# Forty tokens an expert instead of 48, and the second pair's weights fetched during attention

## The chip, the core and the metric

The kernel runs on one core of a Trainium2 chip. The metric is the device time of one execution in microseconds (us). Names of engines: PE is TensorE (its matmuls; PEld its weight loads), DVE is VectorE, ACT is ScalarE, POOL is GpSimd, SP is SyncE, which here only issues DMAs.

## The reference

Two blocks follow each other on 256 tokens of width 1024, all in float32. The first has two layers of retention and stick-breaking attention with a dense SwiGLU; the change does not touch it. The second has two layers of mixed attention followed by a mixture of 32 experts (4 groups of 8). Each token chooses the best group and in it the two best experts:

```python
lg = einsum('td,dg->tg', t, rg_w) + rg_b
g_star = argmax(lg, -1)
le = (einsum('td,gde->tge', t, re_w) + re_b) of the chosen group
top_v, top_i = lax.top_k(le, 2)
gate = p_top * softmax(top_v) at top_i
for g in range(4):
    h = silu(einsum('td,edf->tef', t, w_gate[g])) * einsum('td,edf->tef', t, w_up[g])
    y = y + einsum('tef,efd->td', h * gate[:, g, :, None], w_down[g])
```

Every expert has 1024 x 256 gate, 1024 x 256 up and 256 x 1024 down weights, 1 MB (1.049 million bytes) each. Worked out from the reference's own inputs, the fullest expert gets 30 tokens in the first of these two layers and 33 in the second.

## The kernel before

The experts are worked off in 16 pairs ("duos", `d` from 0 to 15), two experts at a time, side by side on the two halves of TensorE's columns. A pass serves at most `TAKEN_SLOTS` tokens of each expert; `npass` says at run time how many passes the fullest expert needs, and the kernel is built for up to `PASSES` of them, in nested branches. With at most 48 tokens each, one pass is enough.

In a pass PE does this for each pair (`moe_pass`, line 1720):

- `gather` (L1734): multiplies the tokens (in a high and a low part) with 0/1 columns of `pick`, `TAKEN_SLOTS` columns an expert, for a later group of pairs. The 16 pairs form five groups (`GROUP_DUOS`), of 2, 4, 4, 4 and 2 pairs; the columns of a whole group go through one matmul. A group of four pairs takes 32 matmuls of 8 x 48 = 384 columns, a group of two 32 matmuls of 4 x 48 = 192 columns. Group 0 is gathered before pair 0; group 1 during pairs 0 (24 matmuls) and 1 (8); group 2 during pairs 2 to 5, group 3 during 6 to 9 (8 matmuls in each pair), group 4 during 10 to 13 (8 in each, 192 columns). ACT (L2197) and DVE (L2915) copy the results to `XG`.
- `gate_up2` (L1775): the gate and up products of the pair, 16 matmul calls, which the profile counts as 32.
- `turn_hidden` (L1788) turns the hidden rows, ACT copies them (L2224); `turn_picks` (L1747, L1749) turns the picks for the scatter; `down2` (L1801) is the down product; `scatter` (L1815) adds the pair before to the tokens' sums in PSUM.

The gate and up matmuls always read 64 columns an expert (`SLOTS`), of which the last ones belong to the next expert and meet zero picks later.

**Weights.** A pair needs six units of 1 MB. There are 12 slots for them, six for even pairs (`ring`, slots 0 to 5) and six for odd ones: slots 6, 7 and 10 in `high`, slots 8, 9 and 11 in `more_slots`, a piece of the `arena`. For pairs 0 to 3 the gate and up weights come in halves of 0.5 MB (rows 0 to 3 and 4 to 7 of the eight), for the rest whole. SP issues every load of a weight, in order, on one queue. `expert_loads` (L1092) waits before each unit until PE has read what the slot held: for `d >= 2` the unit of pair `d - 2`; for pair 0, in the ring, the unit of `v1` or `w_o_2` of the attention; and before the first load of pair 1 there is one wait, on `z_dve` (L1105), DVE's signal that the second half of `Z`, the attention's normed output, is written. All ten loads of pair 1 (8 halves and 2 down units) stand behind it. `high` holds the high parts of the attention's weights until then (`high_part2`), and the arena holds the attention's tensors (`mqT`, `mkT`, `dqT`, `dkT` and others) in the places in which the expert stage keeps its own.

Of the kernel before, what the change touches and what calls it, by code (L numbers as in the profile page):

```python
# [32 lines left out]
P = 128  # L33
# [3 lines left out]
D = 1024  # L37
# [60 lines left out]
TAKEN_SLOTS = 48  # L98
# [238 lines left out]
def build(nc, src, out, debug=None):  # L337
# [7 lines left out]
    with ctx:  # L345
# [188 lines left out]

        arena_at[0] = moe_at
# [30 lines left out]
        pickT = carve(2, SEQ)  # L566
        Y = T8.rearrange("p k n -> p (k n)").rearrange("p (a n) -> p a n", a=2)
        H_high = carve(TT, D)
# [4 lines left out]
        more_slots = carve(EXPERT_SLOTS - RING - HIGH, UNIT)  # L573
        earlier_twins = len(twins)
        twin_of(gate_parts_flat, ident_moves, pick_flat, pickT, H_high)
# [5 lines left out]
        sg = carve(2, EH)  # L581
        hh = carve(2, EH)
        hT = carve(2, 2 * P)
# [340 lines left out]
        def expert_slot(name, d, i, h=0):  # L924

            if name == "down":
                return ring[:, 4 + i, :] if d % 2 == 0 else high[:, 2, :] if i == 0 else more_slots[:, 2, :]
            if d < HALVED:
                slot = ring[:, 2 * h + i, :] if d % 2 == 0 else high[:, i, :] if h == 0 else more_slots[:, i, :]
                return slot.rearrange("p (s k n) -> p s k n", s=2, k=KT // 2)  # L930
            slots = ring[:, 2 * i:2 * i + 2, :] if d % 2 == 0 else high[:, 0:2, :] if i == 0 else more_slots[:, 0:2, :]
            return slots.rearrange("p s (k n) -> p s k n", k=KT)

# [9 lines left out]
        def _(sp_):  # L943
# [116 lines left out]
            def wait_released2(key, l):  # L1060
                sp_.wait_ge(*released2(key, l))
# [3 lines left out]
            for l in range(LAYERS):  # L1065
# [25 lines left out]

                def expert_loads(pass_):  # L1092
                    passes = None
                    for d in range(DUOS):
                        if d == DUOS // 2 and pass_ == 0:
                            passes = passes_known()
                        for n, key in enumerate(duo_units(0, d)):
                            if d >= 2:
                                wait_released2(held_by(pass_, d - 2, units2[key]), l)
                            elif pass_ > 0:  # L1100
# [795 lines left out]
        def _(act):  # L1896
# [179 lines left out]
            for l in range(LAYERS):  # L2076
# [173 lines left out]
                def squares_of_rows():  # L2250

                    for t in range(TT):
                        act.wait_ge(mean_in.sem, mean_in.at(l, t + 1))
                        nc.scalar.activation(more_slots[:, 0, t * D:(t + 1) * D], H[:, t, :], ACT.Square,
                                             bias=less_mean[:, t:t + 1],
                                             accum_out=square_sum[:, t:t + 1]).then_inc(squares_in.sem, 1)
                    if l < LAYERS - 1:
                        high_parts2(0, 2, l + 1)
# [927 lines left out]
```

## Time and profile before

| | |
|---|---|
| median of 3 runs | 1687.33 us (1685.79 to 1688.91) |
| span of the profiled execution | 1686.1 us |
| what lies around the span | 1.2 us, taken as the median less the span; the profiled execution has no other time |
| PE busy | 1656.0 us, 98% of the span |
| DVE, ACT, POOL busy | 858.9, 652.7, 171.1 us |
| moved by DMA | 396.64 MB, 235 GB/s on average |
| expert stages | from about 1028 to 1262 us and from about 1438 to 1673 us |

The busy share of an engine over the whole span says little here, as the stages have different limits. A busy PE only says that matmuls were in flight. The views that bear on the change are the ones with times: the chain of waits, the stretches with the share of the DMA engines, SP's issues, and the time from a load's issue to its landing.

### The profile page before, as it was taken

How to read it: one execution, taken by the hardware profiler on the slowest of the kernel's cores; microseconds unless marked ns; L12 is line 12 of the kernel's file. 1: busy time of each engine (PE TensorE's matmuls, PEld its weight loads, DVE VectorE, ACT ScalarE, POOL GpSimd, SP SyncE). 2: the span in 40 equal slices, each digit the busy share in tenths (PEclk: the TensorE clock that was granted, in tenths of full speed). 3: DMA queues.
4: the chain of work that ended last, by engine and by line, in shares of the span. 5: the costliest groups of instructions: out<-in, count | busy, mean ns of one | idle time of the engine just before them, and what ended most of it. 6: DMA issues, size and time to landing. Idle time of an engine off the chain costs nothing. (4 is left out here: it accounts for less than half of the span.)

```text
span 1686.1 us, 23648 instructions
## 1 busy us (share of the span) xinstructions
PE 1656.0 (98%) x9477; PEld 1260.6 (75%) x9477; DVE 858.9 (51%) x1418; ACT 652.7 (39%) x920; POOL 171.1 (10%) x242
## 2 busy tenths in 40 slices
PE   9999999999999999999999999999999999999996
PEld 6888879999798887999988975444548887544453
DVE  6466564444646556544457856322127785532223
ACT  4465444343446554433344553111115554211111
POOL 2020001111102000111111040000002122000000
PEclk9999999999999999999999999999999999999998
DMA  8544545553754454555366528999995624999995
GB/s 316 176 149 144 181 150 185 190 185 114 242 183 132 143 181 169 175 188 186 124 203 192 170 76 312 409 423 423 423 394 180 194 101 136 355 425 423 423 423 211
DMA packets 156285, 396.64 MB, mean 235 GB/s; under 512 B 20496, under 2 KB 85008, under 8 KB 135696
## 3 DMA queue, kind: packets, MB, share of 16 engines
q1 hardware_dynamic: 156176, 395.18, 64.4%
q8 instruction: 69, 1.13, 0.3%
q14 instruction: 40, 0.33, 0.1%
HBM read 394.10 MB, written 1.05 MB: 234 GB/s over the span
## 5 line engine op out<-in xcount | busy, mean ns | idle before, releaser
L918 PE MATMUL ps<-split,split 128*128 128x256 f32 (+3 forms) x1872 | 631.2, 337 | 2.1 <-ACT split L1920 1.0
L922 PE MATMUL ps<-split,split 128*128 128x256 f32 (+3 forms) x1872 | 627.7, 335 | 0.2
L919 PE MATMUL ps<-split,split 128*128 128x256 f32 (+3 forms) x1872 | 623.7, 333 | 0.0
L896 DVE TENSOR_TENSOR split<-ring,split 128x2048 fp32r<-128x2048 f32 x136 | 313.6, 2313 | 253.0 <-ACT split L889 252.8
L918 PEld LDWEIGHTS ps<-split,split 128*128 128x128 f32 x1872 | 351.5, 188 | 37.4 <-DVE split L876 2.1
L922 PEld LDWEIGHTS ps<-split,split 128*128 128x128 f32 x1872 | 351.7, 188 | 35.8 <-DVE split L2302 1.3
L919 PEld LDWEIGHTS ps<-split,split 128*128 128x128 f32 x1872 | 352.9, 189 | 33.0 <-issue 0.5
L889 ACT ACTIVATE split<-ring 128x2048 fp32r<-128x2048 f32 x136 | 260.2, 1915 | 278.1 <-PE ps L922 269.4
L1775 PE MATMUL ps<-ring,arena 128*64 128x512 f32 x512 | 112.8, 592 | 0.0
L2952 DVE SCALAR_TENSOR_TENSOR arena<-arena,ps 128x256 f32<-128x256 f32 x32 | 15.4, 481 | 167.4 <-ACT arena L2219 131.9
L1775 PE MATMUL ps<-high,arena 128*64 128x512 f32 x256 | 98.8, 592 | 0.0
L1775 PE MATMUL ps<-arena 128*64 128x512 f32 x256 | 98.8, 592 | 0.0
L911 DVE TENSOR_TENSOR split<-ring,split 128x1536 fp32r<-128x1536 f32 (+3 forms) x44 | 80.7, 1852 | 25.7 <-ACT split L905 25.5
L2964 DVE TENSOR_TENSOR split<-ps,split 128x512 fp32r<-128x512 f32 x64 | 44.3, 692 | 95.8 <-ACT split L2226 95.8
L1775 PEld LDWEIGHTS ps<-ring,arena 128*64 128x64 f32 x512 | 38.5, 137 | 70.1 <-issue 70.1
L2219 ACT ACTIVATE arena<-ps 128x256 f32<-128x256 f32 x32 | 12.3, 384 | 200.5 <-PE ps L1775 200.5
L905 ACT ACTIVATE split<-ring 128x1536 fp32r<-128x1536 f32 (+3 forms) x44 | 67.7, 1546 | 49.1 <-PE ps L922 46.0
L2226 ACT ACTIVATE split<-ps 128x512 fp32r<-128x512 f32 x64 | 38.2, 597 | 111.7 <-PE ps L1801 111.7
L1775 PEld LDWEIGHTS ps<-high,arena 128*64 128x64 f32 x256 | 30.8, 137 | 62.0 <-issue 62.0
L1815 PE MATMUL ps<-split,split 128*128 128x512 f32 x240 | 62.5, 399 | 0.0
L1801 PE MATMUL ps<-ring,arena 128*64 128x512 f32 x256 | 58.5, 598 | 0.9 <-ACT arena L2224 0.9
L1801 PE MATMUL ps<-high,arena 128*64 128x512 f32 x128 | 58.2, 597 | 1.1 <-ACT arena L2224 0.9
(262 smaller groups left out, 1771.1 us busy)
## 6 DMA issues: line engine op xcount, KB each, us to landing
ring<-in_w_in SPq DMA_DIRECT2D x52, 1024.0 KB, 5.1
ring<-in_w_gate_up SPq DMA_DIRECT2D x44, 1024.0 KB, 5.3
ring<-in_expert_w_down SPq DMA_DIRECT2D x32, 1024.0 KB, 11.7
ring<-in_expert_w_gate SPq DMA_DIRECT2D x24, 1024.0 KB, 11.3
ring<-in_expert_w_up SPq DMA_DIRECT2D x24, 1024.0 KB, 13.4
ring<-in_w_down SPq DMA_DIRECT2D x22, 1024.0 KB, 4.9
ring<-in_w_in SPq DMA_DIRECT2D x28, 768.0 KB, 4.6
high<-in_expert_w_down SPq DMA_DIRECT2D x16, 1024.0 KB, 11.9
```

The lines of the kernel that those rows point to most:

```text
L889: nc.scalar.activation(split(high[:, n % HIGH, :]), ring[:, units[key], :], ACT.Copy).then_inc(high_done.sem, 1)
L896: nc.vector.tensor_tensor(split(slot), slot, split(high[:, n % HIGH, :]), ALU.subtract).then_inc(low_done.sem, 1)
L905: nc.scalar.activation(split(high[:, n % HIGH, 0:used(key)]), ring[:, units2[key], 0:used(key)], ACT.Copy).then_inc(high2_done.sem, 1)
L911: nc.vector.tensor_tensor(split(slot), slot, split(high[:, n % HIGH, 0:used(split2[n])]), ALU.subtract).then_inc(low2_done.sem, 1)
L918: nc.tensor.matmul(acc, sh, mh, start=start, stop=False)
L919: nc.tensor.matmul(acc, *second, start=False, stop=False)
L922: return nc.tensor.matmul(acc, *third, start=False, stop=stop)
L1775: mm = nc.tensor.matmul(acc[i * SLOTS:(i + 1) * SLOTS, :].rearrange("p (s n) -> p s n", s=2), XG[g % 2][:, at:at + SLOTS], w_[:, :, k % w_ ...
L1801: mm = nc.tensor.matmul(bank2(("yg", 0, d, half))[i * SLOTS:(i + 1) * SLOTS, :], hT[:, d % 2, j * P + i * SLOTS:j * P + (i + 1) * SLOTS], ...
L1815: mm = nc.tensor.matmul(bank2(("sc", 0, i)), moe_split(pickT[:, d % 2, t * P:(t + 1) * P]), moe_split(Y[:, part, half * 512:(half + 1) * 5 ...
L2226: nc.scalar.activation(moe_split(Y[:, 0, half * 512:(half + 1) * 512]), content_p("yg", d, half), ACT.Copy).then_inc(y_high.sem, 1)
L2964: nc.vector.tensor_tensor(moe_split(Y[:, 1, cols]), acc, moe_split(Y[:, 0, cols]), ALU.subtract).then_inc(y_low.sem, 1)
```

## The change

`TAKEN_SLOTS` goes from 48 to 40. So the gathers have 8 x 40 = 320 or 4 x 40 = 160 columns, an expert's column in `XG` starts 40 floats (160 bytes) after the one before in place of 48 (192 bytes), and `PASSES` goes from 6 to 7.

`more_slots` becomes three single units in the arena. Two (slots 8 and 9) lie where the attention keeps `mqT` and `mkT`, which PE reads last for the scores of the last pair of heads; the third (slot 11) begins at `dkT`. `sg`, `hh` and `hT` lie in `dqT`'s place, `pickT` and `H_high` behind slot 11.

The loads of pairs 0 and 1 are now issued together, by `first_duos`; the wait on `z_dve` is gone. Slots 8, 9 and 11 wait for the last scores, slots 6, 7 and 10 for the output unit `w_o_2` whose high part they held. Pairs from 2 on are loaded as before.

```diff
-TAKEN_SLOTS = 48
+TAKEN_SLOTS = 40
...
+        scored_at = mqT.offset
+        scored_end = dqT_flat.offset
+        dilated_at = dkT_flat.offset
...
-        pickT = carve(2, SEQ)
-        H_high = carve(TT, D)
...
-        more_slots = carve(EXPERT_SLOTS - RING - HIGH, UNIT)
+        assert arena_at[0] <= scored_at
+        arena_at[0] = scored_at
+        more_slots = [carve(UNIT) for _ in range(2)]
+        assert arena_at[0] <= scored_end
+        arena_at[0] = scored_end
         sg = carve(2, EH)
         hh = carve(2, EH)
         hT = carve(2, 2 * P)
+        assert arena_at[0] <= dilated_at
+        arena_at[0] = dilated_at
+        more_slots.append(carve(UNIT))
+        pickT = carve(2, SEQ)
+        H_high = carve(TT, D)
...
+                def first_duos():
+                    at = {}
+                    for d in range(2):
+                        for key in duo_units(0, d):
+                            at.setdefault(units2[key], []).append(key)
+                    def load(slot):
+                        for key in at[slot]:
+                            sp_.dma_start(into2(key), source2(key, l)).then_inc(landed[slot], 16)
+                    wo_of_ring = {units2[k]: k for k in dense[len(dense) - 4:]}
+                    wo_of_high = {split2.index(k) % HIGH: k for k in dense[len(dense) - 4:]}
+                    for slot in range(2):
+                        wait_released2(dense[len(dense) - RING + slot], l)
+                        load(slot)
+                    scored = ("S", JOB_PAIRS[-1][1], 0)
+                    sp_.wait_ge(filled[banks2[scored]], banks2.before(scored, l) + 1)
+                    for slot in (8, 9, 11):
+                        load(slot)
+                    for slot in (2, 3, 4, 5):
+                        wait_released2(wo_of_ring[slot], l)
+                        load(slot)
+                        for n in range(HIGH):
+                            if wo_of_high[n] == wo_of_ring[slot]:
+                                load((6, 7, 10)[n])
...
-                            elif d == 0:
-                                wait_released2(dense[len(dense) - RING + units2[key]], l)
-                            elif n == 0:
-                                sp_.wait_ge(z_dve.sem, z_dve.at(l, 1))
```

On SP, at the end of the attention of the first of the two layers, the order before has the last two ring loads of pair 0 and then all of pair 1 behind `z_dve` (`filled3` is PE's end of a PSUM bank, `unit_read2` its count of units read):

```order
L1106 DMA ring<-in_expert_w_down 128x2048 [waits unit_read2]
L1106 DMA ring<-in_expert_w_down 128x2048 [waits filled3]
L1106 DMA high<-in_expert_w_gate 128x1024 [waits z_dve]
L1106 DMA high<-in_expert_w_up 128x1024
L1106 DMA high<-in_expert_w_gate 128x1024
L1106 DMA high<-in_expert_w_up 128x1024
L1106 DMA arena<-in_expert_w_gate 128x1024
L1106 DMA arena<-in_expert_w_up 128x1024
L1106 DMA arena<-in_expert_w_gate 128x1024
L1106 DMA arena<-in_expert_w_up 128x1024
L1106 DMA high<-in_expert_w_down 128x2048
L1106 DMA arena<-in_expert_w_down 128x2048
```

In the change the arena loads of pair 1 stand ahead of the third ring slot, and the `high` loads between the ring loads of pair 0:

```order
L1114 DMA arena<-in_expert_w_gate 128x1024 [waits filled6]
L1114 DMA arena<-in_expert_w_up 128x1024
L1114 DMA arena<-in_expert_w_gate 128x1024
L1114 DMA arena<-in_expert_w_up 128x1024
L1114 DMA arena<-in_expert_w_down 128x2048
L1114 DMA ring<-in_expert_w_gate 128x1024 [waits unit_read2]
L1114 DMA ring<-in_expert_w_up 128x1024
L1114 DMA ring<-in_expert_w_gate 128x1024 [waits unit_read2]
L1114 DMA ring<-in_expert_w_up 128x1024
L1114 DMA high<-in_expert_w_gate 128x1024
L1114 DMA high<-in_expert_w_up 128x1024
L1114 DMA ring<-in_expert_w_down 128x2048 [waits unit_read2]
```

So five loads moved ahead of the last two w_o units, and the other five go out with them.

On PE nothing moves; the gathers get narrower. Around the start of pair 0, before (gathers of group 0, picks, gate and up of pair 0, gathers of group 1):

```order
L1734 MATMUL ps<-split_57 128x192
L1734 MATMUL ps<-split_57,split_50 128x192
L1747 MATMUL ps<-split_57 128x128
L1749 MATMUL ps<-split_57 128x4
L1747 MATMUL ps<-split_57 128x128
L1749 MATMUL ps<-split_57 128x4
L1775 MATMUL ps<-ring,arena 64x512 x16
L1734 MATMUL ps<-split_57 128x384
L1734 MATMUL ps<-split_57,split_50 128x384
```

and in the change (`split_58` is the arena's second twin, for `pickT` and `H_high`):

```order
L1774 MATMUL ps<-split_57,split_58 128x160
L1774 MATMUL ps<-split_57,split_50 128x160
L1787 MATMUL ps<-split_57 128x128
L1789 MATMUL ps<-split_57 128x4
L1787 MATMUL ps<-split_57 128x128
L1789 MATMUL ps<-split_57 128x4
L1815 MATMUL ps<-ring,arena 64x512 x16
L1774 MATMUL ps<-split_57,split_58 128x320
L1774 MATMUL ps<-split_57,split_50 128x320
```

The count and order of the matmuls are the same; 192 became 160 and 384 became 320.

## Rows read from the trace of the kernel before

**Rows 1.** The page: rate of the DMA engines in 40 slices of 42.2 us.

```profile
GB/s 316 176 149 144 181 150 185 190 185 114 242 183 132 143 181 169 175 188 186 124 203 192 170 76 312 409 423 423 423 394 180 194 101 136 355 425 423 423 423 211
```

**Rows 2.** Chain that ended last, second expert layer: start us, us, what.

```profile
1472.03 6.87 PE ps L1775 x32
...
1486.53 6.87 PE ps L1775 x32
...
1612.10 0.24 PE ps L1788 x2
1612.36 0.39 ACT arena L2224
...
1658.17 6.87 PE ps L1775 x32
```

**Rows 3.** Stretches: engines' busy us (count), granted clock, DMA share, GB/s.

```profile
1385.00:1390.00 5.00, 5.00 (x40) 3.96 (x36) 2.86 (x14) 3.54 (x15) 4.40 (x7) 1.00 0.00 0
1430.00:1435.00 5.00, 5.00 (x23) 2.99 (x23) 2.93 (x24) 0.00 (x0) 0.00 (x0) 0.66 0.99 288
1445.00:1450.00 5.00, 5.00 (x26) 2.19 (x23) 4.43 (x16) 0.47 (x2) 0.00 (x0) 1.00 0.68 179
1630.00:1635.00 5.00, 5.00 (x26) 1.99 (x24) 1.22 (x2) 0.60 (x1) 0.00 (x0) 1.00 1.00 421
```

**Rows 4.** Timeline of SP, both expert layers: start us, us to issue, load.

```profile
1022.59 0.44 SPq L1106 DMA_DIRECT2D arena<-in_expert_w_down  x1
1035.49 0.33 SPq L1106 DMA_DIRECT2D ring<-in_expert_w_gate  x1
...
1228.95 0.43 SPq L1106 DMA_DIRECT2D arena<-in_expert_w_up  x1
...
1445.58 0.33 SPq L1106 DMA_DIRECT2D ring<-in_expert_w_gate  x1
...
1639.04 0.43 SPq L1106 DMA_DIRECT2D arena<-in_expert_w_up  x1
```

**Rows 5.** DMAs issued about 1022.6, 1228.9 and 1639.0 us: KB each, us to landing.

```profile
arena<-in_expert_w_down SPq DMA_DIRECT2D x1, 1024.0 KB, 15.3
...
arena<-in_expert_w_up SPq DMA_DIRECT2D x1, 1024.0 KB, 19.0
...
arena<-in_expert_w_up SPq DMA_DIRECT2D x1, 1024.0 KB, 17.1
```

**Rows 6.** Timeline of PE, first expert layer, start of pair 15.

```profile
1248.12 0.61 PE L1775 MATMUL ps<-high,arena 128*64 128x512 f32 x1
```

**Rows 7.** Pair 4's last up and its downs, issued about 1069, 1076, 1479, 1486 us.

```profile
ring<-in_expert_w_up SPq DMA_DIRECT2D x1, 1024.0 KB, 14.2
...
ring<-in_expert_w_down SPq DMA_DIRECT2D x2, 1024.0 KB, 11.7
...
ring<-in_expert_w_up SPq DMA_DIRECT2D x1, 1024.0 KB, 13.4
...
ring<-in_expert_w_down SPq DMA_DIRECT2D x2, 1024.0 KB, 9.7
```

**Rows 8.** Timeline of PE: gathers of group 0 and of group 1, first and last.

```profile
1438.08 0.28 PE L1734 MATMUL ps<-split 128*128 128x192 f32 x1
...
1441.21 0.28 PE L1734 MATMUL ps<-split 128*128 128x192 f32 x1
...
1449.19 0.34 PE L1734 MATMUL ps<-split,split 128*128 128x384 f32 x1
...
1451.99 0.34 PE L1734 MATMUL ps<-split,split 128*128 128x384 f32 x1
```

**Rows 9.** Lines by form, PE, 0 to 900 us: busy us, mean ns of one.

```profile
L918 PE MATMUL ps<-split,split 128*128 128x512 f32 x688 | 273.3, 397 | 1.4 <-ACT split L1920 1.0 <-issue 0.3
...
L918 PE MATMUL ps<-split,split 128*128 128x256 f32 x832 | 233.7, 281 | 0.0
```

**Rows 10.** The page's groups: weight loads of the gate and up products.

```profile
L1775 PEld LDWEIGHTS ps<-ring,arena 128*64 128x64 f32 x512 | 38.5, 137 | 70.1 <-issue 70.1
```

More of the change, by code:

```diff
@@ L572, in build @@
         XG = [carve(XG_end + SLOTS - TAKEN_SLOTS) for _ in range(2)]
-        more_slots = carve(EXPERT_SLOTS - RING - HIGH, UNIT)
+        assert arena_at[0] <= scored_at
[3 more added lines that the diff above has]
+        arena_at[0] = scored_end
+        sg = carve(2, EH)
+        hh = carve(2, EH)
+        hT = carve(2, 2 * P)
+        assert arena_at[0] <= dilated_at
[3 more added lines that the diff above has]
+        H_high = carve(TT, D)
         earlier_twins = len(twins)
-        twin_of(gate_parts_flat, ident_moves, pick_flat, pickT, H_high)
+        twin_of(gate_parts_flat, ident_moves, pick_flat)
+        twin_of(pickT, H_high)
         moe_twins = twins[earlier_twins:]
@@ L579, in moe_split @@
             return split(view, moe_twins if view.tensor.name == arena.name else None)
-        sg = carve(2, EH)
-        hh = carve(2, EH)
-        hT = carve(2, 2 * P)
         Z = carve(TT, D)
@@ L926, in expert_slot @@
             if name == "down":
-                return ring[:, 4 + i, :] if d % 2 == 0 else high[:, 2, :] if i == 0 else more_slots[:, 2, :]
+                return ring[:, 4 + i, :] if d % 2 == 0 else high[:, 2, :] if i == 0 else more_slots[2]
             if d < HALVED:
-                slot = ring[:, 2 * h + i, :] if d % 2 == 0 else high[:, i, :] if h == 0 else more_slots[:, i, :]
+                slot = ring[:, 2 * h + i, :] if d % 2 == 0 else high[:, i, :] if h == 0 else more_slots[i]
                 return slot.rearrange("p (s k n) -> p s k n", s=2, k=KT // 2)
-            slots = ring[:, 2 * i:2 * i + 2, :] if d % 2 == 0 else high[:, 0:2, :] if i == 0 else more_slots[:, 0:2, :]
+            slots = ring[:, 2 * i:2 * i + 2, :] if d % 2 == 0 else high[:, 0:2, :] if i == 0 else late_slots
             return slots.rearrange("p s (k n) -> p s k n", k=KT)
+        late_slots = arena[:, scored_at:scored_end].rearrange("p (s n) -> p s n", s=2)
         def expert_landed(key, l, pass_):
@@ L1096, in expert_loads @@
                             passes = passes_known()
-                        for n, key in enumerate(duo_units(0, d)):
+                        if pass_ == 0 and d < 2:
+                            if d == 0:
+                                first_duos()
+                            continue
+                        for key in duo_units(0, d):
                             if d >= 2:
                                 wait_released2(held_by(pass_, d - 2, units2[key]), l)
-                            elif pass_ > 0:
+                            else:
                                 wait_released2(held_by(pass_ - 1, DUOS - 2 + d, units2[key]), l)
-                            elif d == 0:
-                                wait_released2(dense[len(dense) - RING + units2[key]], l)
-                            elif n == 0:
-                                sp_.wait_ge(z_dve.sem, z_dve.at(l, 1))
                             sp_.dma_start(into2(key), source2(key, l)).then_inc(landed[units2[key]], 16)
@@ L2253, in squares_of_rows @@
                         act.wait_ge(mean_in.sem, mean_in.at(l, t + 1))
-                        nc.scalar.activation(more_slots[:, 0, t * D:(t + 1) * D], H[:, t, :], ACT.Square,
+                        nc.scalar.activation(more_slots[0][:, t * D:(t + 1) * D], H[:, t, :], ACT.Square,
                                              bias=less_mean[:, t:t + 1],
```

## The prediction

> **What bounds the kernel now.** I first read the page's rate of the DMA engines [rows 1]. It stands at 423 GB/s in the slices of the two expert stages and at half of that or less in the attentions, so weights could come early. Is the expert stage held by them? The chain of waits [rows 2] says no: there it is PE all the way, one pair every 1486.53 - 1472.03 = 14.50 us, with no DMA in it. But the stretches [rows 3] show the DMA engines 100% busy as well, at 421 to 423 GB/s from the third pair on. A pair needs 6 x 1.049 = 6.29 MB, which at 424 GB/s takes 14.84 us. So the loads are 0.34 us a pair slower than PE and live on a lead. The reader should see how much of it is left at the end, pair 15.
>
> Times from here on are counted from s, the issue of pair 2's first load, which is the moment at which PE has read half of pair 0's gate and up weights: 1035.49 us in the first expert layer, 1445.58 in the second [rows 4].
>
> - PE begins gate and up of pair 15 at 1248.12 and 1658.17 [rows 6, 2]: s + 212.63 and s + 212.59.
> - The last load that it needs (arena, up) is issued at 1228.95 and 1639.04 [rows 4] and takes 19.0 and 17.1 us [rows 5]. It lands at 1247.95 and 1656.14: s + 212.46 and s + 210.56.
>
> The lead left is 0.17 us in the first layer and 2.03 us in the second. **The first layer stands at the edge at which both bind; in the second PE binds by 2 us.** Where do the 1.9 us between the layers come from? Pair 1's last load in the first layer is issued at 1022.59 and takes 15.3 us [rows 4, 5], so it lands 2.4 us after s, and pair 2 queues behind it. In the second layer the queue is nearly empty at s (share 0.68 and 179 GB/s in the 5 us from 1445 [rows 3]). At pair 4's last up unit the first layer is 14.2 - 13.4 = 0.8 us late, at its two down units 11.7 - 9.7 = 2.0 us [rows 7]. So about 0.8 us is the late start, and 1.2 us is lost once inside pair 4, for a reason that I don't see.
>
> **The change part by part.**
>
> *Narrower gathers, 384 to 320 columns.* 3 groups x 32 = 96 matmuls a layer, all after s. They start (1451.99 - 1449.19)/16 = 175 ns apart [rows 8], which is 0.456 ns a column. The mean durations of like matmuls give (397 - 281)/256 = 0.453 ns a column [rows 9]. 64 columns fewer are 29 ns; 96 x 29 ns = 2.8 us of PE a layer. From pair 2 to 9 eight of them lie in each pair, so PE comes to 14.50 - 0.23 = 14.27 us a pair.
>
> *192 to 160 columns.* 64 matmuls a layer, 32 of them before s. These start (1441.21 - 1438.08)/28 = 112 ns apart [rows 8]; by columns alone it would be 192 x 0.456 = 88 ns. So something else sets their pace, and narrower ones gain nothing: I take 0. The bounds are 0 and 32 x 0.456 = 15 ns each, 0.5 us a layer ahead of s. The Trainium skill (TensorE: Matmul & The Clock Gate, "Back-to-back issue gap") gives a gap of N/2.4 + 2.5 ns at full clock, hence 82.5 ns for 192 columns and 69 for 160, which speaks for a gain; the row's 112 ns disagrees.
>
> *Copies to XG.* ACT and DVE copy 17% less a gather. Both sit beside PE here (DVE 1.22 and ACT 0.60 of 5 us [rows 3]); 0.
>
> *Lost cover.* In pairs 2 to 9 a gather of four matmuls stands between turning the hidden rows and the down products, and hides ACT's copy of them. Where it is absent (pairs 10 on) the copy of 0.39 us shows in the chain behind the 0.24 us of turning [rows 2]. A gather of 4 x 146 = 0.58 us and the picks behind it still cover it; 0.
>
> *Early loads of pair 1.* Ten loads, 6.29 MB, 15 us of DMA time at 424 GB/s. The five to the arena go out at the last scores of the attention, into stretches at 0 GB/s [rows 3], the others with the last w_o units. What else is on SP's queue? Only pair 0's loads, which now wait behind the scores; those end before the first w_o unit is read, on which the next ring load waited anyway. Nothing on PE waits for these loads earlier than before, so in the attention they are worth 0. Their worth is what is no longer in the queue at s: in both layers pair 2 then meets an idle queue, as in the second layer now.
>
> *The rest.* The 12 slots are released by the same matmuls. From pair 2 on each load's issue stays or comes earlier, and the queue, once filled, stays filled; its end is then s plus a constant. The seventh pass is code that isn't reached: at most 33 tokens go to an expert.
>
> **The sum.** In both layers pair 15 starts at the later of two: PE ready at s + 212.6 - 2.8 = s + 209.8; last load landed at s + 210.56, plus about 0.15 us until PE starts (0.17 in the first layer now), s + 210.7. **The loads bind now.** PE waits some 0.9 us before pair 15, and each layer gains 212.6 - 210.7 = 1.9 us: 3.8 us in all. Pair 14 had more lead and doesn't wait. Behind pair 15 nothing changes. The profiled execution goes from 1686.1 to 1682.3 us of span; the median of the runs lies 1.2 us above the span, so I say 1683.5.
>
> **The rivals.**
>
> 1. *The 1.2 us stay.* The late step inside pair 4 of the first layer has nothing to do with the early loads (it comes 50 us after s). If one layer's loads lose it again, that layer gains 0.7 instead of 1.9: 1684.7. For it: it is in the trace, and I can't name a cause that goes away. Against: the second layer doesn't have it. 0.22.
> 2. *PE decides.* If the loads run a little better than in the second layer before, both layers gain the full 2.8: 1687.3 - 5.6 = 1681.7. Against: the rate has been flat at 421 to 423 GB/s; the lead needed is 0.9 us a layer. 0.10.
> 3. *The 192-column gathers shrink as well.* Then s itself comes 0.45 us earlier in each layer: 1683.5 - 0.9 = 1682.6. The skill's rule for the gap, cited above, would have it so. 0.08.
> 4. *The early loads don't advance the queue* in the first layer: its lead stays at 0.17 us, it gains 0.1, the second 1.9: 1685.3. Against: pair 2's loads queue behind pair 1's for 2.4 us. 0.07.
> 5. *Slower: weights at 160-byte steps.* Gate and up take their stationary columns from XG, and an expert's now begin at multiples of 160 bytes, not 192. A weight load takes 137 ns [rows 10], two of them are due each 6.87/16 = 0.43 us [rows 2]. Up to 215 ns a load it costs nothing; were it to double to 274, each of the 16 steps of a pair would grow by 0.12 us, 1.9 us a pair and 60 us over 32 pairs: 1744. For it: nothing in this trace has such a step. Against: it needs a load 1.6 times as long, for the same 64 columns. 0.05.
> 6. *Slower: a second pass.* An expert with 41 to 48 tokens would need one, about 230 us (16 pairs at 14.3): 1914. By the counts it isn't so. 0.01.
>
> What moves all of these by chance is the clock: from 1430 to 1435 the granted clock was 0.66 on average, so parts at the lower level (1.2 GHz) though PE was busy just before, and the first layer has no such dip in its like stretch. It costs up to 5 x 0.34 = 1.7 us, and may go or come twice; that isn't the change's doing.
>
> **How the numbers follow.** The forecast has 0.42, the rivals 0.53, and 0.05 is for what I haven't thought of, half of it slower. A difference under 0.2%, 3.4 us, can't be told from none here, so the line lies at 1684.0, half a microsecond above my forecast. Of the forecast's 0.42, given the run-to-run spread of a microsecond, about two thirds fall below it (0.28); rivals 2 and 3 almost wholly (0.17), of rival 1 a quarter (0.05): faster 0.50. The rest of the forecast and of rivals 1 and 4, with some of the unknown, make 0.42 for the same. Slower is 5, 6 and half of the unknown: 0.08. The range reaches from rival 2's 1681.7 less 0.3 to rival 4's 1685.3 plus 1.0 for spread and clock: 1681.4 to 1686.3.
>
> **What would show it.** Right: gathers at 146 ns, 112 ns unchanged for the narrow ones; a stretch of 14.27 us a pair up to pair 9; DMA engines idle at s in both layers; the last up unit of pair 15 landing near s + 210.6 in both; and a wait of PE before pair 15 of 0.5 to 1 us for a landing, the one DMA in the chain. Pair 15 then starts at s + 210.7. Wrong: no wait there and a start at s + 209.8 (rival 2); a landing near s + 211.8 in one layer (rival 1); weight loads above 137 ns (rival 5); or any wait for a landing before pair 0 or 1, which would mean that the early loads were in the way of pair 0's.

## The result and the profile after

The changed kernel took 1689.45 us in the median (1688.28 to 1691.89, 7 runs), the kernel before 1685.79 us beside it (7 runs): ratio 1.0021, 95% interval 1.0012 to 1.0031. It is 3.7 us slower. 1683.5 us were forecast, from 1687.3 for the kernel before: 3.8 us less were forecast, 3.7 us more were measured. A second set of 12 runs (e4 below) gave 1.0026 [1.0017, 1.0035]. The profiled execution took 1688.28 us, with a span of 1686.5.

Page of the changed kernel, rate of the DMA engines in 40 slices, beside [rows 1]:

```profile
GB/s 317 180 144 150 174 150 194 180 193 106 250 175 141 139 185 159 177 195 179 123 204 194 167 188 217 407 421 421 421 393 159 198 109 250 239 421 420 421 421 223
```

Pair 1's loads have moved forward (slices 24 and 35 rise from 76 to 188 and from 136 to 250), and the flat part reads 421, where it read 423.

Timeline of SP in the changed kernel: pair 2's first load (that is s) and pair 15's last up unit, both expert layers, beside [rows 4]:

```profile
1034.57 0.33 SPq L1146 DMA_DIRECT2D ring<-in_expert_w_gate  x1
...
1225.11 0.43 SPq L1146 DMA_DIRECT2D arena<-in_expert_w_up  x1
...
1446.20 0.33 SPq L1146 DMA_DIRECT2D ring<-in_expert_w_gate  x1
...
1637.68 0.43 SPq L1146 DMA_DIRECT2D arena<-in_expert_w_up  x1
```

The DMA view about the two up loads, KB and us to landing, beside [rows 5]:

```profile
arena<-in_expert_w_up SPq DMA_DIRECT2D x1, 1024.0 KB, 22.1
...
arena<-in_expert_w_up SPq DMA_DIRECT2D x1, 1024.0 KB, 21.3
```

So they land at 1247.2 and 1659.0: s + 212.6 and s + 212.8, where s + 210.56 was forecast for both. They are issued 2 to 3 us earlier against s than before (190.5 and 191.5, before 193.5), and land no earlier. Timeline of PE at pair 15, beside [rows 6]; in brackets the idle time ahead and what ended it:

```profile
1247.30 1.08 PE L1815 MATMUL ps<-high,arena 128*64 128x512 f32 x1 [2.57 <-SPq L1164]
...
1248.17 1.06 PE L1815 MATMUL ps<-high,arena 128*64 128x512 f32 x1
...
1659.08 0.62 PE L1815 MATMUL ps<-high,arena 128*64 128x512 f32 x1 [1.62 <-SPq L1164]
```

TensorE is ready at 1244.7, s + 210.2, and waits 2.57 us; in the second layer 1.62 us. The name in the bracket is SP's queue, yet both waits end within 0.15 us behind the landing. Matmuls that take 0.59 us take 1.06 right behind the first wait.

Pair 15 isn't the only one that waits. Waits of PE in the second expert layer (us in all, times, longest; L1164 is the wait before pair 15):

```profile
PE ps L1815 <- SPq L1164: 1.6, 1, 1.6
PE ps L1841 <- ACT arena L2264: 0.9, 4, 0.2
PE ps L1815 <- DMA arena<-in_expert_w_up: 0.4, 1, 0.4
PE ps L1815 <- DMA ring<-in_expert_w_up: 0.4, 1, 0.4
```

The two last are waits for a landing before pairs 13 and 14; in the first layer pair 14 waits 0.30 us. So the lead was used up before pair 15: with these, TensorE waits 2.9 and 2.6 us for loads in the two layers. The four waits of 0.2 us for ACT's copy are there in the kernel before as well.

Stretches of the changed kernel (us, busy us and counts, granted clock, DMA share, GB/s):

```profile
1246.00:1251.00 5.00, 3.70 (x12) 1.32 (x14) 0.17 (x1) 0.00 (x0) 0.00 (x0) 0.66 0.99 409
1446.20:1451.20 5.00, 5.00 (x27) 2.53 (x24) 4.19 (x16) 1.00 (x2) 0.00 (x0) 1.00 0.77 194
```

The clock is at its lower level, 1.2 GHz, for 3.4 us from 1246.9 on, the end of the wait. Lines by form, PE, and one PE row with 20 gathers, beside [rows 8, 9, 10]:

```profile
L1774 PE MATMUL ps<-split,split 128*128 128x320 f32 x192 | 38.6, 329 | 0.0
L1774 PE MATMUL ps<-split,split 128*128 128x160 f32 x128 | 16.5, 280 | 0.8 <-DVE split L2906 0.8
```

```profile
1026.79 3.77 PE L1774 MATMUL ps<-split,split 128*128 128x160 f32 x32 [0.41 <-DVE split L2906]
...
1449.53 3.18 PE L1774 MATMUL ps<-split,split 128*128 128x320 f32 x20
```

```profile
L1815 PEld LDWEIGHTS ps<-ring,arena 128*64 128x64 f32 x512 | 38.1, 137 | 72.0 <-issue 72.0
```

TensorE's own part came as forecast: up to pair 9 a pair takes 14.25 us, forecast 14.27. The wide gathers start (3.18 - 0.31)/19 = 151 ns apart, forecast 146, before 175; the narrow ones (3.77 - 0.28)/31 = 113 ns, unchanged; weight loads take 137 ns. PE is busy 1650.5 us, 5.5 less than before.

So three things were to be explained: loads that end 2 us late, the clock behind the wait, and, since the waits of some 5 us only cancel the saving, 3.7 us more that had no place yet.

### The profile page after: what moved, and what is told of

Its sections match the earlier page's. It is cut to its first block and busy times, and to the rows that moved or that the text cites. A ratio compares the mean times of both kernels' runs of the same rounds, so it can differ in the third digit from the quotient of the medians.

```text
span 1686.5 us, 23650 instructions
## 1 busy us (share of the span) xinstructions
PE 1650.5 (98%) x9477; PEld 1253.9 (74%) x9477; DVE 857.0 (51%) x1420; ACT 650.9 (39%) x920; POOL 171.2 (10%) x242
## 3 DMA queue, kind: packets, MB, share of 16 engines
HBM read 394.10 MB, written 1.05 MB: 234 GB/s over the span
## 5 line engine op out<-in xcount | busy, mean ns | idle before, releaser
L929 PEld LDWEIGHTS ps<-split,split 128*128 128x128 f32 x1872 | 351.5, 188 | 37.1 <-issue 2.1
L933 PEld LDWEIGHTS ps<-split,split 128*128 128x128 f32 x1872 | 351.7, 188 | 36.0 <-DVE split L2342 1.3
L930 PEld LDWEIGHTS ps<-split,split 128*128 128x128 f32 x1872 | 352.9, 189 | 33.0 <-issue 0.5
L1815 PE MATMUL ps<-high,arena 128*64 128x512 f32 x256 | 100.3, 599 | 4.6 <-SPq L1164 4.2
L916 ACT ACTIVATE split<-ring 128x1536 fp32r<-128x1536 f32 (+3 forms) x44 | 67.7, 1547 | 49.4 <-PE ps L933 46.3
L1774 PEld LDWEIGHTS ps<-split,split 128*128 128x128 f32 x320 | 43.9, 191 | 24.5 <-issue 24.5
```

The source lines that it names most:

```text
L916: nc.scalar.activation(split(high[:, n % HIGH, 0:used(key)]), ring[:, units2[key], 0:used(key)], ACT.Copy).then_inc(high2_done.sem, 1)
L929: nc.tensor.matmul(acc, sh, mh, start=start, stop=False)
L930: nc.tensor.matmul(acc, *second, start=False, stop=False)
L933: return nc.tensor.matmul(acc, *third, start=False, stop=stop)
L1774: mm = nc.tensor.matmul(acc[:, j * SEQ:j * SEQ + XG_cols[g]].rearrange("p (e n) -> p e n", n=TAKEN_SLOTS), moe_split((H_high, H_low)[part] ...
L1815: mm = nc.tensor.matmul(acc[i * SLOTS:(i + 1) * SLOTS, :].rearrange("p (s n) -> p s n", s=2), XG[g % 2][:, at:at + SLOTS], w_[:, :, k % w_ ...
```

## The experiments

Every ratio is to the kernel before, timed beside it on the same chip; the groups e, f, i and j were timed apart from each other. A landing or a wait comes from one execution each. "Packet" is the mean duration of the 8 KB packets in the DMA records from 1080 to 1240 us; a load of 1 MB is 128 of them. "Landing" is that of pair 15's last up unit, first and second layer, from s. "Lost to the clock" is (1 - mean granted clock) x span, a mean over all runs of a kernel. It is more than the clock cost: every traced execution ends with 7 to 10.5 us at 1.2 GHz in which TensorE has nothing to do, 3.5 to 5.3 us of the figure. In the changed kernel (PE's busy time is the number behind the comma):

```profile
1677.00:1686.40 9.40, 0.00 (x0) 0.00 (x0) 5.03 (x5) 1.18 (x2) 3.58 (x3) 0.50 0.31 118
```

So only differences between kernels count. By the scatter of the runs each mean is uncertain by 0.3 to 0.9 us.

**The halves of the change apart.** e1 is the kernel before, unchanged; e4 the changed kernel, unchanged. e2 and e3 have one half each:

```
e2: before, TAKEN_SLOTS = 40          e3: changed, TAKEN_SLOTS = 48
```

> The kernel before, unchanged, for a trace on the same chip as the next three. Theory L (the queue of expert loads binds): from s (issue of pair 2's first load) to the landing of pair 15's last up unit it takes about 212.5 us in both layers on this chip too, and the 210.56 us of the second layer in the first trace was a favourable case; 8 KB packets take about 0.314 us as in the changed kernel if that figure belongs to the chip, 0.312 if it belongs to the kernel. Rival E (the change itself makes the loads slower): 210.5 to 212.5 here, 212.6 to 212.8 only with the new arena or the early loads. Ratio to before 1.000 under both.

> The kernel before with 40 tokens an expert and nothing else: arena and loads as before. Theory L: PE is ready for pair 15 at about s + 209.8 and waits 2.5 to 3 us for the last up unit in both layers, so nothing is gained, and where the wait lets the clock drop 1 to 2 us are lost: ratio 1.000 to 1.002, like the changed kernel. Rival E (the early loads or the arena cost the time): 40 tokens alone gain 2 to 5 us, ratio 0.997 to 0.999.

> The changed kernel with TAKEN_SLOTS back at 48: early loads and new arena, gathers as wide as before. Theory L: PE is ready for pair 15 at s + 212.6, waits 0 to 0.3 us, no clock drop there; ratio 0.999 to 1.000 (the first layer gains at most the 0.2 us at which it stood). Rival E: as slow as the changed kernel, ratio 1.001 to 1.003.

> The changed kernel unchanged, on the same chip as the three before. Theory L: waits of 2.4 to 2.9 us before pair 15 in both layers, ratio 1.001 to 1.003. If the first comparison was chance, the ratio is within 0.0005 of 1.

| | ratio | packet, ns | landing | waits before pair 15 | lost to the clock |
|---|---|---|---|---|---|
| e1 before | 1.0003 [0.9994, 1.0011] | 312.3 | 212.15, 211.46 | 0, 0 | 7.4 |
| e2 only 40 | 1.0021 [1.0012, 1.0030] | 314.1 | 212.21, 212.56 | 2.05, 1.60 | 9.1 |
| e3 only early | 1.0013 [1.0004, 1.0023] | 314.1 | 213.27, 212.57 | 0.98, 0.28 | 8.6 |
| e4 both | 1.0026 [1.0017, 1.0035] | 314.1 | 213.05, 212.37 | 2.16, 1.63 | 9.4 |

Each half alone is slower. e1 also shows that the second layer's landing at s + 210.56, on which the forecast stood, was one execution's luck: here it is s + 211.46. e3 missed its expectation: it waits 0.98 us in one layer and its ratio is 1.0013, where at most 0.3 us and 1.000 were expected. And the packets fall into two classes. e2 changes nothing in the loads, but takes 314.1 ns a packet. What it does change is where things lie: with XG shorter, the three arena slots begin at other bytes. Adding up the layout gives, for the first byte of the slots in a partition:

| | ring | high | arena |
|---|---|---|---|
| before | 128 past a multiple of 256 | 32 past one of 64 | on multiples of 256 |
| e2 | same | same | 64 past one of 256 |
| e3, e4, changed | same | same | 32 past one of 64 |

Load by load (128 packets each, in order of time), e1 has six of the twelve loads of two pairs at 309 to 312 ns (arena's gate and up, high's and arena's down, and the first gate and up of the next pair, into ring) and the other six at 313 to 316; in e4 all twelve take 313 to 317. That gave theory A: where the slots begin sets the packets' time.

**Only the addresses.** Four kernels:

```
f1 (before)     +        carve(8)
                         more_slots = carve(EXPERT_SLOTS - RING - HIGH, UNIT)
f2 (changed)    +        carve(24)
                         mqT = carve(HM, SEQ)
f3 (f2)         +        minus_half, lstat, stat      (128 bytes, ahead of ring)
                         ring
                +        high                         (right behind ring)
f4 (changed)    -HALVED = 4
                +HALVED = 2
```

> The kernel before with one edit: 8 unused floats ahead of the three arena slots, so these slots begin 32 bytes further on (byte 184608 of a partition in place of 184576, a multiple of 256). Nothing else differs, no load, no order, no count of tokens. Theory A (where a slot begins sets how long its packets take): the 8 KB packets of the expert stream take 314.2 ns in the mean in place of the 312.3 ns of the kernel before, as they did in the only-40, only-early and changed kernels; the last up load lands some 1.0 us later than s+211.5 to 212.1, at s+212.4 to 213.1, about where TensorE becomes ready (s+212.6), so the time rises by 0 to 2 us, ratio 1.000 to 1.0012. Rival (the packets are slower because of what else the changed kernels do on the SBUF ports or queues): 312.3 ns again, landing at s+211.5 to 212.1, ratio 1.0000.

> The changed kernel with one edit: 24 unused floats ahead of mqT in the arena, which put the three arena slots on bytes 179968, 188160 and 202496 of a partition, all multiples of 256 as in the kernel before (the changed kernel has 179872, 188064, 202400, multiples of 32 alone). Theory A: packets back to 312.3 ns, the last up load at s+211.5 to 212.0 in place of s+212.4 to 213.1, the wait before pair 15 shrinks from 1.6 to 2.6 us to 1.3 to 1.8 us a layer, and the ratio to the kernel before falls from 1.0024 to 1.000 to 1.0015. Rival (the early loads or the 40 tokens slow the stream, not the addresses): packets at 314.2 ns, wait and ratio as in the changed kernel.

> The changed kernel with the arena pad of the run before, and ring and high moved as well: three small tensors (128 bytes) are laid ahead of ring and high right behind it, so that all twelve expert slots begin on multiples of 256 (ring was on a multiple of 128 alone, high of 32 alone). Theory A: in the kernel before the arena slots, on multiples of 256, took 309.5 ns a packet, ring 312.5 and high 315; with all on 256 all take about 309.5 to 310, the stream ends 1.3 to 1.6 us earlier than that of the kernel before, at s+210 to 210.7, and TensorE (ready at s+209.9 to 210.2) waits 0 to 0.7 us; the ratio is 0.997 to 0.999, the first kernel that gets the saving of the 40 tokens. If the addresses of ring and high do nothing: as the run before, s+211.5 to 212.0 and 1.000 to 1.0015.

> The changed kernel with HALVED = 2 in place of 4: only the first two pairs fetch their gate and up weights in halves, so pairs 2 and 3 load with 8 KB packets, in 24 transfers fewer of half the size; the addresses of the slots stay at multiples of 32. The halved loads of pairs 2 and 3 make the first 12 MB of the stream take 37.7 us where the same bytes take 29.7 us later on. Theory L (the loads set the end of the experts; the 40 tokens are gained on TensorE and lost in a wait for the last weights): the stream can start 3 us later since whole slots must come free, and ends 4 to 5 us earlier against TensorE; no wait before pair 15; TensorE's full 2.8 us a layer show, ratio 0.996 to 0.9985, unless TensorE now waits before pair 2 for a whole load, which would show as a wait there. Rival (something else than the loads, such as later scatter work or a slower layer ahead of the experts, costs the change its gain): the wait before pair 15 goes and the ratio stays at 1.001 or over.

| | ratio | packet, ns | landing | waits before pair 15 | lost to the clock |
|---|---|---|---|---|---|
| f1 | 1.0011 [1.0002, 1.0020] | 314.3 | 213.05, 212.95 | 0.60, 0.48 | 6.7 |
| f2 | 1.0014 [1.0002, 1.0025] | 312.3 | 211.95, 211.0 | 2.10, 1.22 | 8.9 |
| f3 | 0.9947 [0.9934, 0.9960] | 309.4 | 210.15, 209.34 | 0.74, 0 | 6.7 |
| f4 | 1.0004 [0.9995, 1.0012] | 314.6 | 211.35, 210.34 | 1.84, 0.85 | 8.3 |

Stretches 1080 to 1230 us of the kernel before, of f1, of f2 and of f3, in this order (the last number is GB/s):

```profile
1080.00:1230.00 150.00, 149.33 (x731) 73.84 (x728) 34.40 (x74) 26.55 (x52) 0.00 (x0) 1.00 1.01 423
```

```profile
1080.00:1230.00 150.00, 149.33 (x734) 74.35 (x730) 34.43 (x74) 26.85 (x53) 0.00 (x0) 1.00 1.01 421
```

```profile
1080.00:1230.00 150.00, 149.10 (x741) 73.58 (x741) 35.16 (x78) 26.91 (x54) 0.00 (x0) 1.00 1.01 423
```

```profile
1080.00:1230.00 150.00, 149.11 (x738) 72.00 (x736) 34.20 (x74) 26.27 (x52) 0.00 (x0) 1.00 1.01 427
```

Theory A holds in all three steps, f1 to f3. f1 moves the three arena slots, and with them the small buffers that lie behind them (`sg`, `hh`, `hT`, `Z`), by 32 bytes and slows the stream from 423 to 421 GB/s, so that TensorE, with its 48 tokens, waits. f2 brings the changed kernel back to 423; its ratio, 1.0014, is below e4's 1.0026, but the intervals overlap. f3 puts all twelve slots on multiples of 256 and reaches 427; all twelve loads then take 309 to 311 ns a packet. f3's row at pair 15 of the first layer shows the wait that is left, 0.74 us; the second layer has none:

```profile
1238.48 0.61 PE L1816 MATMUL ps<-high,arena 128*64 128x512 f32 x1 [0.74 <-SPq L1165]
```

f3 gained more than I expected: its s is 1028.17 where f2's is 1032.80, so 4.6 us come ahead of the first expert layer. They can be placed. Busy time of the instructions that read or write the split tiles, which hold the high and low parts of the operands, up to the start of the experts, in f2 and then in f3 (PE's is the first number behind the comma):

```profile
0.00:1027.00 1027.00, 880.62 (x5106) 774.36 (x5107) 393.28 (x249) 328.75 (x246) 50.12 (x88) 1.00 0.53 178
```

```profile
0.00:1022.00 1022.00, 875.41 (x5103) 778.91 (x5103) 393.31 (x248) 328.69 (x246) 50.01 (x88) 1.00 0.54 179
```

The matmuls of the split products take 5.2 us less. Their operands lie in ring, high and T8, at other addresses in f3; which of the moves did it wasn't tried. No landing of an expert weight has a part in this.

f4 fell short: two pairs less in halves end the stream 1.7 to 2.0 us earlier, not the 4 to 5 expected. In the first layer its first 16 MB have landed 46.3 us after s, against 48.6 in e4, so most of the slow start isn't the 4 KB packets. Its wait stays, at 1.84 and 0.85 us, and so does the loss.

**The parts again, where the loads don't bind; and the clock.** i1 is the kernel before with ring and high on 256, i2 the same with 40 tokens (and 48 floats ahead of the arena slots, to keep them on 256), i3 is f3 with HALVED = 2. i4 is the changed kernel with

```
                         acc = bank2(("gu", 0, d))
                +        if pass_ == 0 and d == DUOS - 1:
                +            keep_running(acc, 8)
```

> The kernel before with ring and high moved to multiples of 256 as in f3 (its arena slots are there already); 48 tokens, late loads. Theory A with L: packets 309.4 ns, the last up load at s+209.5 to 210.3; TensorE, ready at s+212.6, never waits and sets the end of the experts as in the kernel before, so the layers of experts gain nothing, and all that is gained is what f3 gained ahead of the experts (s came 4.6 us earlier than in f2): ratio 0.9965 to 0.998. Rival (f3's gain is the addresses alone, the 40 tokens and early loads give nothing even there): as f3, 0.994 to 0.9955.

> The kernel before with 40 tokens in place of 48, the loads of pairs 0 and 1 where they were, and all twelve slots on multiples of 256. Theory (the early loads are worth nothing, TensorE's saving shows once the loads end before it): as f3, waits of 0 to 0.8 us before pair 15, ratio 0.994 to 0.9955, some 0.003 below i1. Rival (the early loads bring something where the loads don't bind): 0.996 or over, between i1 and f3.

> f3 (the changed kernel, all slots on 256) with HALVED = 2 in place of 4. f4 against e4 ended the stream 1.7 to 2.0 us earlier against s; with it f3's 210.15 and 209.34 become 208 to 208.5, behind which TensorE (s+209.9 to 210.2) never waits. f3 has one wait of 0.74 us left in one layer, so 0 to 0.8 us are to be had: ratio 0.9935 to 0.9947, not told apart from f3 by more than that. If halving costs anything else (a wait for a whole load in pairs 2 or 3) it is f3's ratio or above.

> The changed kernel with eight matmuls of no use (213 ns each, 1.7 us) ahead of the gate and up projections of pair 15, in the place where TensorE waits 1.6 to 2.6 us for the last weights, so that it idles 0 to 0.9 us there; nothing is computed differently. Theory (the wait lets the clock fall, and that is part of the loss): the half-clock stretch of 3.4 us behind the wait of the first layer of experts goes from the records, the mean clock rises from 0.9944 to about 0.9953, and the ratio falls from 1.0026 to 1.0010 to 1.0020. Rival (the clock's stretches have nothing to do with this wait, or cost nothing): mean clock and ratio as in the changed kernel, 1.0024 or over.

| | ratio | packet, ns | landing | waits before pair 15 | lost to the clock |
|---|---|---|---|---|---|
| i1 before, 256 | 0.9965 [0.9952, 0.9979] | 309.4 | 210.01, 209.61 | 0, 0 | 7.7 |
| i2 only 40, 256 | 0.9946 [0.9932, 0.9959] | 309.4 | 210.28, 209.96 | 0.59, 0.29 | 9.1 |
| i3 changed, 256 | 0.9943 [0.9929, 0.9957] | 309.8 | 209.34, 208.75 | 0, 0 | 8.4 |
| i4 changed, 8 more | 1.0000 [0.9991, 1.0009] | 314.1 | 213.11, 212.23 | 0, 0 | 6.0 |

On good addresses the 40 tokens seem to pay: i2 is 0.0019 below i1, 3.7 us in the medians (1680.57 and 1676.85), but these are five runs each and the intervals overlap. i1's own gain, 0.0035, isn't one of the expert loads: TensorE waits for none of them in i1 or in the kernel before. Its s is 1029.73 where it was 1035.49, and its split products take 5.2 us less up to there, as in f3. The early loads add nothing that can be told: f3 and i2 agree within 0.0001. At the same packet time (e1 and f2, both 312.3 ns) the loads land 0.2 and 0.5 us earlier with them.

i4 does more work than e4, ends its stream at the same time, and is 4.5 us faster, where 1 to 2.7 us were expected. Timeline of PE in i4: the eight matmuls bridge the wait and pair 15 runs at full speed.

```profile
1245.31 1.90 PE L1215 MATMUL ps<-ones 128*128 128x512 bf16 x8
1247.13 0.64 PE L1817 MATMUL ps<-high,arena 128*64 128x512 f32 x1
```

But something else went too. Timeline of PE in e4 at the start of the second attention (transposes L1524, matmuls of no use L1215), and then in i4:

```profile
1269.54 1.17 PE L1524 MATMUL ps<-ident,H 128*128 128x128 f32 x8 [1.31 <-DVE H L3050]
1272.86 1.25 PE L1215 MATMUL ps<-ones 128*128 128x512 bf16 x5 [2.15 <-issue]
1273.95 1.87 PE L1524 MATMUL ps<-ident,H 128*128 128x128 f32 x8
```

```profile
1268.73 1.16 PE L1524 MATMUL ps<-ident,H 128*128 128x128 f32 x8 [1.43 <-DVE H L3052]
1269.73 1.24 PE L1215 MATMUL ps<-ones 128*128 128x512 bf16 x5
1270.81 1.04 PE L1524 MATMUL ps<-ident,H 128*128 128x128 f32 x8
```

In e4 TensorE idles 2.15 us ahead of five matmuls that wait for no one, and the clock's second half-speed stretch begins behind it (1274.0; the eight transposes take 1.87 us, not 1.05). The changed kernel has 1.26 us there, e2 1.48, f2 1.92, f3 2.38, f4 1.60, i2 2.12, i3 1.71. The kernel before, e1 and i4 have none; e3, f1 and i1 have none there either, but idle 2.4 to 2.7 us, put down to issue, one step earlier, ahead of the transposes. These transposes and the five matmuls are the first code behind the jump over the passes that aren't run. The half-speed stretch doesn't follow the idle time each time: it does in e4 and i2; in f3, f4 and i3 it begins ahead of it, 0.6 to 1 us behind the wait before the transposes; the changed kernel's first trace, e2 and f2 have none.

**Only the place of the code.** j1 puts 56 matmuls into passes that are never reached (the expectation has the code lie where i4's does, but i4 has only its eight more ahead of it); j2 leaves the seventh pass out; j3 is i3 with j1's edit:

```
j1, j3          +        if pass_ > 0 and d == DUOS - 1:
                +            keep_running(acc, 16 if pass_ == 1 else 8)
j2              -PASSES = -(-SEQ // TAKEN_SLOTS)
                +PASSES = 6
```

> The changed kernel with matmuls added only in passes 2 to 7 of the experts, which are never run: 16 in pass 2 and 8 in each later one. No instruction that is executed differs; only the place in memory of TensorE's code behind the first expert layer is the same as in i4. In the changed kernel and in e2, e4, f2, f3 TensorE idles 1.3 to 2.4 us (put down to issue) some 24 to 27 us behind the start of pair 15, in the first transposes of the second attention, and mostly falls to half clock behind it; the kernel before and i4 have no such idle time. Theory C (that idle time is the fetch of code behind the jump over the unreached passes and hangs on where the code lies): it goes, and with it a stretch of half clock; the wait before pair 15 of 1.6 to 2.6 us and its own half-clock stretch stay; mean clock .9944 rises to about .9955, the ratio falls from 1.0026 to 1.0005 to 1.0015. Rival (i4 lost that stall since TensorE had no idle time before pair 15): stall, clock and ratio as in the changed kernel.

> The changed kernel with the code of the seventh pass left out (PASSES = 6; at most 33 tokens go to an expert, so passes beyond the first are not run in either). TensorE's code behind the first expert layer begins some 600 instructions earlier. Theory C: the idle time put down to issue behind the jump changes its place or size, in a way that I can't say ahead (0 to 2.4 us), and the ratio with it, 1.0005 to 1.0026; the wait before pair 15 stays at 1.6 to 2.6 us. Rival (the seventh pass itself costs, by its length): the stall is gone, 1.0005 to 1.0015. If neither stall nor ratio moves, the code has no part in it.

> i3 (the changed kernel, all slots on multiples of 256, two halved pairs) with the unreached matmuls of j1. i3 has an idle time of 1.7 us put down to issue at 25 us behind the start of pair 15 and a half-clock stretch of 6.8 us behind it. Theory C: both go, 1.0 to 1.7 us and 1.7 to 3.4 us: ratio 0.9943 falls to 0.9915 to 0.993, below every kernel so far. Rival: as i3, 0.9935 to 0.995.

| | ratio | median, us | landing | waits before pair 15 | lost to the clock |
|---|---|---|---|---|---|
| j1 | 0.9995 [0.9986, 1.0004] | 1685.47 | 212.71, 213.08 | 2.74, 1.61 | 6.6 |
| j2 | 0.9993 [0.9982, 1.0004] | 1684.30 | 210.9, 212.19 | 1.37, 1.61 | 7.2 |
| j3 | 0.9925 [0.9912, 0.9939] | 1673.41 | 209.25, 208.66 | 0, 0 | 7.0 |

j1 executes what e4 executes, waits 2.74 and 1.61 us before pair 15 (e4: 2.16 and 1.63), and is 0.0031 faster, with intervals 0.0013 apart. It was timed beside the kernel before, not beside e4. Timeline of PE in j3, where i3 had 1.71 us of idle time ahead of the five matmuls:

```profile
1259.80 1.17 PE L1525 MATMUL ps<-ident,H 128*128 128x128 f32 x8 [1.43 <-DVE H L3053]
1260.80 1.24 PE L1216 MATMUL ps<-ones 128*128 128x512 bf16 x5
1261.88 1.06 PE L1525 MATMUL ps<-ident,H 128*128 128x128 f32 x8
```

The idle time ahead of the five matmuls, the stall, is gone in all three kernels. That unreached code, more of it (j1) or less (j2), changes it, and with it the time, is shown; that it is the fetch of code behind the jump is the reading of "issue" that fits, and is argued. The DMA records have packets of instructions, but they don't settle it: one of 16 KB starts at 1270.1 in e4, just ahead of the stall, and one at a like place in e1 (1270.4) and j1 (1271.6), which have none. Nor is it the whole: j1 and j2 idle 1.95 and 2.36 us ahead of the transposes, put down to DVE, where e4 has 1.31; and f1 and i1, whose code lies as before's, idle 1 us longer there than e1 (2.47 and 2.41 us, put down to issue, where e1 has 1.44 for DVE). The profiled execution of j1 was the slowest of its eleven (1691.91 us, five stretches at half clock), so its trace stands only for the missing stall, not for its time.

j1 also gives the eight matmuls of i4 their share. j1 has none, and waits 2.74 and 1.61 us before pair 15; yet its ratio, 0.9995, is no higher than i4's 1.0000, and it lost 6.6 us to the clock against 6.0 in i4 and 9.4 in e4. So nearly all that i4 gained over e4 goes with the place of the code, and the filled wait brought nothing that can be told.

j3, at 1673.41 us, is the fastest kernel: 12.6 us below the kernel before by the ratio. Its interval overlaps i3's.

## Why the prediction was wrong

- *Gathers save 2.8 us a layer, narrow ones nothing.* Right: 151 ns against 175, 113 ns unchanged, 5.5 us of PE in all, and TensorE ready at s + 210.2 in the first layer, forecast 209.8; in the second at s + 211.3, behind waits of 1.0 us in pairs 12 to 14. Rival 3 didn't come: the narrow gathers stay at 113 ns. The rule that the prediction cites for it (the Trainium skill, TensorE: Matmul & The Clock Gate, "Back-to-back issue gap") is by the page's own words that of an isolated matmul and under-counts for few columns, where weights are loaded as well; the trace agrees, with 113 ns against the rule's 69.
- *Lost cover, copies, weight loads at 160-byte steps, second pass.* Right, all nothing: the waits for ACT are those of before (8 of 0.2 us), LDWEIGHTS 137 ns. Rivals 5 and 6 didn't occur.
- *Early loads.* Right that pair 2 meets an idle queue at s, and that the attention doesn't feel it. Wrong that this brings the first layer's landing forward by 1.9 us: between e1 and f2, whose packets take the same, it is 0.2 and 0.5 us in the two layers, less than executions of one kernel differ.
- ***"The queue, once filled, stays filled; its end is then s plus a constant"*: this step failed,** in its size. The constant was taken from the second layer of one execution, 210.56; another execution of the same kernel has 211.46. And it isn't a constant of the queue: moving the arena slots off multiples of 256 made each packet 0.6% longer (312.3 to 314.1 ns), 1.1 us over the stream of 180 us, an estimate. So in the traces of the changed kernel and e4 the loads end at s + 212.4 to 213.1, and all that TensorE saved is waited away. (One trace with the same addresses, j2, has 210.9 in one layer; why executions of one kernel differ by 1 to 2 us is open.) f2 gives the address its share: 1.1 and 1.4 us of landing, 0.0012 of the ratio (the intervals overlap).
- *"Pair 14 had more lead and doesn't wait": failed.* It waits 0.30 and 0.43 us, and pair 13 0.44 us in the second layer; in e4 both wait some 0.44 us in both layers.
- *"Behind pair 15 nothing changes": failed.* The wait makes TensorE idle and the clock may fall behind it: the waits of 2.57, 2.16, 2.10 and 2.74 us in the first layer (changed, e4, f2, j1) were followed by 3.4 us at 1.2 GHz, those of 2.05 and 1.84 us (e2, f4) weren't. And, independent of the loads, the code behind the expert layer meets a stall of 1.3 to 2.4 us. I dismissed the seventh pass as "code that isn't reached". It isn't, but it moves the code that is. With more unreached code (j1) or without the seventh pass (j2) 0.0031 to 0.0033 come back, 5 us or more.
- *The clock "isn't the change's doing": wrong in part.* The measure above gives 7.3 us for the kernel before, 9.4 for e4, 6.0 for i4 and 6.6 for j1; of each 3.5 to 5.3 us lie in the idle end and cost nothing.
- *The median lies 1.2 us above the span.* Within each run it is 1.8 us, in all kernels; I had set a profiled span against a median of other runs. That median, 1687.33 of three runs, was also high by 1.5 us against the 1685.79 measured beside the change.
- *Rivals.* Rival 1, that one layer's loads lose time inside the stream again, was nearest: both layers did, by 2 us where it has 1.2. None had the change slower for what happened.

The sum for e4 against the kernel before. TensorE's work up to pair 15 is 5.0 us less in both layers together (ready at s + 211.0 and 210.9 where it was 212.6, with 0.87 and 0.89 us of waits in pairs 13 and 14 on the way). The waits for loads are 5.5 us (2.16 + 1.63 before pair 15, and those). The clock adds 2.1 us (9.4 - 7.3), and the stall 1.3 to 2.2. Timeline of PE in e4, the wait before pair 14 of the first layer:

```profile
1230.78 7.09 PE L1815 MATMUL ps<-ring,arena 128*64 128x512 f32 x32 [0.44 <-DMA ring<-in_expert_w_up]
```

That makes +3.9 to +4.8 us; measured are 4.1 (1690.1 - 1686.0). The agreement is partly luck, as traces of one kernel differ in s by 1 to 2 us and the clock's term is uncertain by about a microsecond. Without the stall the change is worth nothing or next to it: ratios 0.9995 and 0.9993 (j1, j2), with intervals that hold 1. With fast addresses as well, two halved pairs and moved code it is 1673.4 us (j3), and 5 us of that gain come from the split products ahead of the experts.

## What to carry to other kernels

Where loads and an engine both stand at the edge, an edit that only makes the engine faster gives nothing until the loads get faster, and an edit that moves a buffer can change the loads' speed too. After a change of layout, look up where the buffers begin, and try multiples of 256 bytes. Here ring and high on them made the kernel before 0.35% faster (i1), more than the change was meant to bring, though through faster matmuls ahead of the experts and not through the loads; the loads' gain shows only where TensorE waits for them (f2, f3). Before a small loss is put down to an edit's work, try the same kernel with unreached code of another length.

## What the runs showed of the hardware

- Packets of 8 KB into SBUF took 309.4 ns in the mean with all twelve slots on multiples of 256 bytes, 312.3 with the arena's three alone on them, and 314.1 to 314.6 with none; the stream ran at 427, 423 and 421 GB/s. Between the kernel before and f1, and between the changed kernel and f2, nothing but places in the arena differs. It doesn't go slot by slot: in e1 high's down slot, 32 bytes past a multiple of 64, is among the fast loads, and in f1, where it lies the same and only the arena slots moved, among the slow ones (309.7 and 315.8 ns in the first layer). How a load's address reaches its neighbours is open.
- The matmuls of the split products, some 5100 up to the start of the experts, were busy 880 us with ring 128 bytes past a multiple of 256 and high 32 bytes past one of 64, and 875 us with both on multiples of 256 (f2 and f3). Which operand matters wasn't tried.
- The same executed instructions with unreached code of another length: 1690.1 us (1.0026) and 1685.5 us (0.9995), with and without an idle time of 2.15 us put down to issue behind a jump.
- Idle time of TensorE of 1.3 to 2.7 us was in several traces followed by a stretch of 3.4 or 6.8 us at 1.2 GHz, but not in all (f2 has 1.92 us with none behind). The clock's figure fell from 9.4 us in e4 to 6.6 with the code moved (j1), and to 6.0 with eight matmuls of no use in the wait before pair 15 (i4), where the stall went too.
